# One expert block more through the stored results: two late blocks in place of three in a mixture-of-experts kernel

## The reference, cut to what matters

```python
scores = jax.nn.sigmoid((t @ w_router).astype(jnp.float32))
...
w = w / w.sum(axis=-1, keepdims=True)
gates = jnp.sum(jax.nn.one_hot(idx, N_EXPERTS, dtype=jnp.float32) * w[..., None], axis=1)
hid = jax.nn.silu(jnp.einsum('nd,edf->enf', t, w_gate_l)) * jnp.einsum('nd,edf->enf', t, w_up_l)
hid = hid * gates.T[:, :, None].astype(hid.dtype)
out = jnp.einsum('enf,efd->nd', hid, w_down_l)
...
xs = xs + g2 * moe_ffn(h, w_router, router_bias, w_gate[l], w_up[l], w_down[l])
```

## Time and profile before

| | us |
|---|---|
| median of 3 runs (826.24 to 828.26) | 827.12 |
| the profiled execution's own time | 822.9 |
| its span, first to last instruction | 821.2 |
| PE busy | 737.5 (90%) |
| DVE busy | 328.8 (40%) |
| ACT busy | 212.1 (26%) |
| POOL busy | 142.0 (17%) |

### The profile page before, as it was taken

The page is one execution under the profiler, slowest core; times in us unless marked ns, Lnnn a source line. Parts: engine busy times, 40 slices in busy tenths (PEclk is TensorE's granted clock), DMA queues, the critical chain, the costliest instruction groups (busy, mean ns, idle before and its releaser), DMA issues. The chain is left out here.

```text
span 821.2 us, 9341 instructions
## 1 busy us (share of the span) xinstructions
PE 737.5 (90%) x3420; PEld 372.3 (45%) x3420; DVE 328.8 (40%) x865; ACT 212.1 (26%) x484; POOL 142.0 (17%) x238
## 2 busy tenths in 40 slices
PE   3699998998998599999999999888799589999994
PEld 0347553455544344443344755345644344444331
DVE  1302534734534553310272262574543645321136
ACT  1310155724023101111222024583301311011121
POOL 2425041220000120000202403222000020000112
PEclk9799999999899699999999999999899879999998
DMA  8994237899500799999997223345330298999961
GB/s 335 389 360 165 103 109 265 314 362 405 218 1 34 309 374 385 417 424 421 379 355 272 103 103 109 131 184 212 116 103 0 83 399 353 410 423 422 423 257 77
DMA packets 54051, 211.54 MB, mean 258 GB/s; under 512 B 7883, under 2 KB 8755, under 8 KB 41715
## 3 DMA queue, kind: packets, MB, share of 16 engines
q1 hardware_dynamic: 40456, 179.33, 55.5%
q10 hardware_dynamic: 7851, 17.70, 5.8%
q0 software_dynamic: 5696, 13.89, 4.8%
HBM read 202.02 MB, written 13.93 MB: 263 GB/s over the span
## 5 line engine op out<-in xcount | busy, mean ns | idle before, releaser
L2142 PE MATMUL bank<-ring,work 128*64 128x512 f32 (+1 forms) x512 | 161.1, 606 | 2.6 <-DVE work L1530 2.0
L2142 PEld LDWEIGHTS bank<-ring,work 128*64 128x64 f32 (+1 forms) x512 | 60.0, 160 | 97.9 <-issue 95.1
L2158 PE MATMUL bank<-ring,xs_tok 128*64 128x512 f32 (+1 forms) x256 | 79.9, 597 | 3.6 <-DVE xs_tok L1541 3.6
L1541 DVE COPY xs_tok<-bank 128x256 f32<-128x256 f32 x22 | 9.3, 424 | 147.1 <-PE bank L2149 147.1
L1795 PE MATMUL bank<-hT,ring 128*128 128x384 f32 x192 | 62.2, 486 | 0.0
L1696 PE MATMUL bank<-ring,cpad 128*32 128x512 f32 x384 | 48.6, 632 | 10.1 <-DMA ring<-in_w_ada_dram 9.4
L1795 PEld LDWEIGHTS bank<-hT,ring 128*128 128x128 f32 x192 | 36.5, 190 | 25.0
L2158 PEld LDWEIGHTS bank<-ring,xs_tok 128*64 128x64 f32 (+1 forms) x256 | 27.9, 157 | 41.1 <-issue 35.4
L1763 PE MATMUL bank<-ring,hT 128*128 128x512 f32 x96 | 43.9, 614 | 2.3 <-ACT hT L799 2.3
L973 ACT ACTIVATE xs_tok<-bank 128x256 f32<-128x256 f32 x22 | 8.5, 385 | 140.7 <-PE bank L2142 140.7
L2049 PE MATMUL bank<-ring,xn 128*128 128x512 f32 x96 | 43.3, 593 | 0.0
(11 more groups left out here) (381 smaller groups left out, 1049.3 us busy)
## 6 DMA issues: line engine op xcount, KB each, us to landing
ring<-in_w_ada_dram SPq DMA_DIRECT2D x48, 1024.0 KB, 7.7
ring<-in_w_gate_dram SPq DMA_DIRECT2D x32, 1024.0 KB, 10.2
ring<-in_w_up_dram SPq DMA_DIRECT2D x32, 1024.0 KB, 14.0
ring<-in_w_down_dram SPq DMA_DIRECT2D x32, 1024.0 KB, 12.1
ring<-in_w_in_dram SPq DMA_DIRECT2D x16, 1024.0 KB, 15.0
ring<-in_w_out_dram SPq DMA_DIRECT2D x8, 1024.0 KB
y_exp<-qkv ACTq DMA_DIRECT2D x16, 512.0 KB, 8.0
xpad<-gate_rows ACTq DMA_DIRECT2D x6, 512.0 KB, 4.9
```

The lines of the kernel that those rows point to most:

```text
L1541: dve.tensor_copy(hidT[:, b, :], bank[2][:, 0:F]).then_inc(s_htc, 1)
L2142: last = mm(bank[b][i * n:(i + 1) * n, :].rearrange("p (i f) -> p i f", i=2), rows_T[:, kt * P + i * n:kt * P + (i + 1) * n], gate_up_of(s ...
L2158: last = mm(bank[5 + hf][i * n:(i + 1) * n, :], hidT[:, b, f * P + i * n:f * P + (i + 1) * n], w[:, f, hf * 512:(hf + 1) * 512], start=f = ...
```

## The change

`LATE` becomes 2. `STORED`, `LATE_RANKS` and all that is derived from them follow: block 8 is now stored to `y_exp` and gathered with the others, and selection products are made for blocks 9 and 10 only.

```diff
--- before.py
+++ after.py
@@ -73,7 +73,7 @@
             for pp in range(len(PAIRS)) for k in range(2)]
 BUFS, HOTS = 4, 5
 uses = lambda n, i: len(range(i, NB, n))
-LATE = 3
+LATE = 2
 SELECTIONS, SLOT_SUMS = NB + 2, NB + 1
 STORED = NB - LATE
 LATE_RANKS = [r for p, part in BLOCKS[STORED:] for r in (RANK_AT[p][k] for k in part)]
```

## The result

| | before | changed |
|---|---|---|
| median, us | 827.69 (826.24 to 828.28, 4 runs) | 839.83 (838.64 to 840.62, 4 runs) |
| profiled execution, its own time and span | 822.9, 821.2 | 840.62, 838.8 |
| TensorE clock granted, mean | 0.966 | 0.946 |

The changed kernel is slower: ratio 1.0139, 95% interval 1.0109 to 1.0169, or 12.1 us where 10.3 were forecast. The two profiled executions are 17.7 us apart, more than the medians, since the one of before is 4.8 us under the median in the table and the one of after is the longest of its runs. So I measure from a mark within each trace: ACT's copies of block 8's result (L980), which the change does not touch. They start 1.13 us later in layer 0 (395.97 against 394.84) and 11.22 us later in layer 1 (788.77 against 777.55).

A forecast was written before the change was run, and what follows sets the result against it. Stored results and their gathers bound the layer ends, tying with PE in layer 0. Layer 0's 5.0, layer 1's 4.3 and the clock's 1.0 us make 10.3, added to 827.1 for 837.4 us; range 831 to 843.

The forecast's parts named there:

- the forecast's own signs of being wrong: Ninth store landing in under 6 us, gathers over 7 us on emptied queues, or PE's sums releasing DVE.
- The bound: Ends of layers: stored results and their gathers decide layer 1; gather chain and PE tie in layer 0.
- The store: Block 8's store, waited for by POOL's gathers: lands in 8.2 us in layer 0, 8.9 us in layer 1.
- The rival of the early store: Block 8's store lands at some 4.5 us, before the weights are through: 828.6 us; chance 0.12.
- The gathers: POOL's sixth result gather lands in 4.9 us, plus 0.4 us in layer 1 for the final norm's load.
- What is queued behind the wait: ACT's weighting, block 9's copies, PE's last down products: these start at 414.3 and 797.7 instead of 408.91 and 792.06.
- The clock: PE idles 6.9 us before the last down products, so its clock falls: 0.5 us a layer, bounds 0 and about 4.
- The products: Six products fewer per layer, 5.2 us of PE; only PE's 0.6 us slack in layer 0 is given back.
- Sum: Both layer ends and clock: 5.0 + 4.3 + 1.0 = 10.3 us slower, 837.4 us forecast.

The follow-up runs named there:

- the wait alone: Kernel before, all 18 products, also storing block 8's result to a spare table and holding POOL's gathers until it landed: 842.5 us, ratio 1.0197.
- the constants: Changed kernel with seven products of constants on PE, into an unread bank, ahead of the last down products: 839.13 us, ratio 1.0126.
- the first experiment: Kernel before without block 8's selection products, block 8 neither stored nor gathered: 826.89 us, ratio 1.0002.
- the weightings moved: Changed kernel with all weightings behind block 10's copies on ACT and tile 0's addition behind the last hidden copy on DVE: 840.16 us, ratio 1.0161.

## Why the prediction was right

The forecast was 837.4 us in 831 to 843; 839.8 us came. The mechanism held, but two of the forecast's own signs of being wrong came up in one layer each: PE's sums released DVE in layer 0, and the last gather took over 7 us in layer 1. By its own steps:

- **The bound** was read rightly: the chain over the stored results sets the end in both layers after the change, in layer 1 straight over the last gather, in layer 0 by way of PE: block 9's copies stand behind the first gathers, and PE's down products and sums behind those copies. The experiment with the wait alone gives the whole loss.
- **The store** (8.2 and 8.9 us taken). Measured from the start of block 8's copies to the first gather, 10.5 us in layer 0 and 10.3 in layer 1, where the forecast has 10.1 and 10.85. The store landed in 8.5 us in layer 0 and in 8.25 us in layer 1. Taking the rows of busy queues and not the idle 2.7 us was the choice that mattered. The rival of the early store is out: no store at L985 landed in under 7.7 us in this trace either. The Trainium skill (DMA: Bandwidth & Descriptors, Queues, rings and completion order) states the round robin between queue rows, packet by packet; that a store therefore gets half the bandwidth at once was the prediction's reading of it, and these landings do not bear that reading out.
- **The gathers** were mis-sized. Layer 0: 4.9 us taken, about 5.5 measured (412.97 to 418.48). Layer 1: 4.9 and 0.4 for the final norm's load, 8.02 measured. That load is the largest single error of the sum: 2.8 us for the gather, of which 1.3 reach the end in the one trace without it. Two slips stand behind the 0.4. The prediction issues the load at 795.8, at the end of the weighting of tile 0, where before it was issued with its start (794.6 by the forecast's own times, ahead of the last gather and not behind it; it was 0.27 us ahead in the trace). And its 6.2 us are no price on quiet queues: the DMA share was 1.02 from 788 to 792 us and 0.28 in the window behind.
- **What is queued behind the wait.** Last down products at 414.3 and 797.7 by the forecast, 19.5 and 20.2 us behind block 8's copies; they came 21.4 and 20.7 us behind them (417.34 and 809.45). They are off the path, as said, but for the clock.
- **The clock** (0.5 us a layer). It fell in both layers, as the rule of the Trainium skill (TensorE: Matmul & The Clock Gate, What's actually happening) had it that the prediction named. By that rule the prediction put the sum 1 to 2 us above its own; the fall came, but its cost stayed near the 1.0 us taken. In layer 1 `late_added(0)` follows the last gather by 6.41 us, exactly as before; in layer 0 by 7.46, and by 6.2 us where constants kept the clock. So the clock put 1.1 to 1.3 us on the path in layer 0 and none in layer 1, 1.0 us in the forecast. That the sum agrees is partly luck: 0.5 us too little in one layer and 0.5 us too much in the other. Released by PE in layer 0, by DVE in layer 1: the forecast had DVE in both.
- **The products.** No effect, said the sum; none, says the experiment. The six products may be worth about 1 us of layer 0 where the clock has made PE the later one (0.9 us in one pair of traces).
- **Sum.** 7.2 and 6.4 us in the two traces against 5.5 and 4.8 with the clock. The excess of 3.3 us is the gathers (0.6 and 2.7 us), the store (0.4 more and 0.6 less) and 0.2 us of rounding and slack. The medians give 12.1 us, so the forecast misses by 1.8 us there and by 3.3 us in the traces; that it looks the better by the medians is not its merit.

## What to carry to other kernels

A result that goes through DRAM costs its store's and its gather's landing under the load of that moment, and a path kept beside it, such as products by selection matrices, pays by the work that it lets overlap, not by what it costs on its own engine: here twelve products fewer gave nothing, and one store more to wait for cost 12 us. Before moving work behind a wait, ask whose idle time it fills now; the same move was neutral in one of these kernels and cost 11.6 us in the other. And look at what lands beside a transfer that is "needed only later": here it lengthened the gather beside it by 2.8 us in a trace, though moving it gave nothing that the medians show.

## What the runs showed of the hardware

- The last of the six gathers landed in 5.0 to 5.7 us with little else queued but its neighbours, in 8.02 and 8.25 us where one load of 512 KB was issued 0.3 us before it (the changed kernel and the wait alone, layer 1), in 6.96 and 7.37 us where that load was issued 0.3 and 1.0 us behind it (the constants and the weightings moved, layer 1), and in 12.4 us among the weight loads.
- A store of 512 KB took 7.7 to 9.0 us to land in the changed kernel's trace, all 18 of them, where stores of the same size with little else queued took 2.7 us.
- The same code between two marks took 344.2 to 347.4 us in different executions, in kernels that do not differ there. A difference of 3 us between two single traces says nothing here unless its place is known.
- Where PE had waited 2.02 us for copies (the first experiment, layer 0), the sixteen down products behind took 5.35 us instead of 3.65. A wait of 1.99 us at the same place in layer 1 of the kernel before with the load moved left them at 3.65 us and the granted clock at 1.00. In the changed kernel, constants in place of the idle stretch gave 1.3 us at that place, and the clock fell at the next wait, of 3.64 us.
